# Hybrid pooling/retention layer on eight cores: input tiles moved into the weight queue, and the last tile's work put in another order

## The chip, the cores and the metric

The kernel runs on the 8 cores of one Trainium2 chip. Every core executes the same program on its own data: one prompt of the batch and 16 of the 128 sample rows. There is no exchange between cores. The metric is the device time of the slowest core in microseconds (us); lower is better.

On each core, TensorE (PE) does the matmuls, VectorE (DVE), ScalarE (ACT) and GpSimd (POOL) do the elementwise work, and transfers are issued from two places: from SyncE (SP, "the hardware queue" below) and from POOL ("the software queue" below, which also converts float32 to bfloat16 on the way).

## What is computed

The reference, cut to the prompt part (the sample part is the same layer with one token and a carried state):

```python
hn = rms_norm(h, norm_w)
u, gp, q, k, v, gr = split(hn @ w_in)            # 1024 -> 6 x 1024
# head group A: trailing means over 2/4/8/16 tokens, minus the token, a linear map per group
pool_o = (window_mean(u) - u) @ w_grp * scale
# head group B: retention in chunks of 128, one fixed decay per head
q, k = rotary(q), rotary(k) * HEAD_DIM ** -0.5
scores = (q @ k.T) * dmask
ret_o = scores @ v + q_dec @ S
S = g ** L * S + k_dec.T @ v
ret_y = rms_norm_per_head(ret_o) * ret_norm_w * silu(gr)
h = h + concat([pool_o * silu(gp), ret_y]) @ w_out
y = rms_norm(h, final_norm_w)
```

`w_in` is 1024 x 6144, `w_out` is 2048 x 1024, and a prompt has 2048 tokens after 16 meta tokens.

## The kernel before

A core cuts its 2048 tokens into 16 tiles of 128 (tile 1 to tile 16). Tile 0 is a small one with the 16 meta tokens and the 16 sample rows. `w_in` lies in HBM as 12 blocks of 128 x 4096 float32 and is kept in SBUF as bfloat16; the order in which blocks are loaded is `WORD = (6, 7, 4, 5, 8, 9, 10, 11, 0, 1, 2, 3)`: two blocks each for k, q, v, gr, u and gp. `w_out` is kept as 16 row blocks `wo0` to `wo15`. The first eight come converted through the software queue; the last eight come as float32 through the hardware queue into a float32 buffer and are multiplied by the retention norm weight on DVE (line 537).

For each tile, `stage_A` loads x, normalises it (ACT square at line 581, a power on POOL at line 553, DVE product at line 584) and `turn` transposes it on PE (line 573). `tile_work` then projects k, q, v, gr and u (line 611, 128x512 matmuls, eight for half a projection) and gp (line 626), rotates k and q on DVE (lines 641 to 646), transposes both, forms scores (791), the state update (697), the retention output (806, 808), its norm and gate (ACT 719, DVE 550 and 728, POOL 553), the pooling matmuls (828 to 835), and the mixing matmuls with `wp0` and `wp1` (744). `wp0` and `wp1` are made on DVE (line 517) from `w_pool` and `pool_scale`. `out_proj` (line 758) multiplies by all of `w_out`; then come the residual add (762), the final norm (764, 553, 767) and the store.

The order is not written by hand. `Prog.schedule` plans it: every operation has a priority (lower goes first), a planned duration and the buffers that it opens, and the planner fixes for each engine one list of instructions, which that engine then executes strictly in order, waiting on semaphores. Transfers are planned at a fixed rate for each queue. Buffers come from pools: 33 of bfloat16 (`b2`), 5 of float32 (`b4`: input tiles, residuals, rotary scratch, staged weights), 4 of PSUM, 3 of rotary tables (`cs`). An instruction that needs a buffer still in use waits, and so does all that stands behind it on its engine or queue.

Around the start, the priorities put the first constant piece and all 12 weight blocks on the software queue at once, and the eight `w_out` blocks behind them. x1 goes on the hardware queue at the start; x2, x3 and x4 go there too, each gated on the landing of an early weight block. `pool_scale` and `w_pool` go on the hardware queue after the tenth weight block. At the end, tile 16 is planned like every other tile, with its second half (scores, retention, pooling) 50 behind its projections in priority.

Of the kernel before, what the change touches and what calls it, by code (L numbers as in the profile page):

```python
# [12 lines left out]
NH = 8  # L13
# [36 lines left out]
class Prog:  # L50
# [102 lines left out]
    def schedule(self):  # L153
# [216 lines left out]
LAG = 2  # L370
HPE, KQPE, YPE = 99, range(99), range(99)
# [6 lines left out]
def build_program():  # L378
# [18 lines left out]
    c_bf = din("c_bf", [128, NBF])  # L397
    c_f32 = din("c_f32", [128, NF32])
    c_cs = din("c_cs", [NT + 1, 128, 192])
# [26 lines left out]
    csr = P.sb("csr", [128, 3 * 192], F32)  # L426
# [3 lines left out]
    P.pool("cs", [csr[:, i * 192:(i + 1) * 192] for i in range(3)])  # L430
# [39 lines left out]
    def copy_any(src, src_r, dst, cols, prio, rows=128, bf=False, scol=0, dcol=0, only=None, **kw):  # L470
        def fa(e):
            return e.activation(out=dst.ap[:rows, dcol:dcol + cols], in_=srcap(), func=AF.Copy)  # L472
# [4 lines left out]
        def srcap():  # L477
# [4 lines left out]
                    [(src, src_r)], [dst], prio, **kw)  # L482
# [16 lines left out]
    dma("sw", lambda: cbf.ap[:, 256:NBF], lambda: c_bf[:, 256:NBF], [], [(cbf, "b")], 128 * (NBF - 256) * 4, -771.5, "uniq")  # L499
    CA, CB = (cbf, "a"), (cbf, "b")  # L500
    LASTW = (win, WORD[-1])
    dma("hw", lambda: cs0.ap, lambda: c_cs[0], [], [cs0], 128 * 768, -700, "uniq")
    dma("hw", lambda: cf.ap, lambda: c_f32[:, :], [(win, WORD[0])], [cf], 128 * NF32 * 4, -690, "uniq")
# [4 lines left out]
    def load_wpool():  # L508
        pscale = P.tile("b4", "pscale")
        dma("hw", lambda: pscale.ap, lambda: pool_scale[0:1, :].broadcast_to([128, D]), [(win, WORD[9])], [pscale], 1 << 19, 30)  # L510
        for i in range(2):
            wpf = P.tile("b4", "wpf")
            dma("hw", lambda wpf=wpf: wpf.ap.rearrange("p (g cc d) -> p g cc d", g=2, cc=2),
                lambda i=i: w_pool[2 * i:2 * i + 2].rearrange("g (cc p) d -> p g cc d", p=128), [(win, WORD[9])], [wpf], 1 << 19, 31)
# [681 lines left out]
```

How the kernel before makes its waits and increments, by code:

```python
        def run(e, name):  # L327
            for o in self.order[name]:
                for s, v in waits[o.i]:
                    e.wait_ge(self.sems[s], v)
                o.fn(e).then_inc(self.sems[o.semname], 16 if o.nbytes else 1)
            if name == "sp":
                for k, v in cnt.items():
                    e.wait_ge(self.sems[k], v)
```

## Time and profile before

| | us |
|---|---|
| median of 4 runs (664.06 to 664.47) | 664.23 |
| the profiled execution | 664.06 |
| its span, slowest core | 662.4 |
| spans of the 8 cores | 656.5 to 662.4 |
| PE busy in the span | 578.8 (87%) |
| DVE / ACT / POOL busy | 354.6 / 183.6 / 122.3 |
| chain that ended last: PE / DMA / DVE | 78% / 8% / 8% |

The profiled execution's time is 1.7 us above its span. All times below are us from the start of the span on the slowest core (core 2). PE is the busiest engine by far, but not evenly so: the page's 40 slices of 16.6 us each show where it is not.

### The profile page before, as it was taken

Reading aid. Unit: us, or ns where it says so; the run is one execution under the profiler, and the core shown is the slowest. Engines: PE = TensorE matmul, PEld = TensorE weight load, DVE = VectorE, ACT = ScalarE, POOL = GpSimd, SP = SyncE. Lnnn points to the kernel's source line nnn. Section 1 sums busy time; section 2 is a strip of 40 time slices with the busy share of each in tenths; the row PEclk is TensorE's granted clock in tenths of the full one; section 3 lists DMA queues with packets and bytes.
Section 4 is the critical chain, followed back from the end, with each engine's and each line's share of the span. In section 5 each row is a group of like instructions: output and inputs, shape, how many; then the busy total and the mean of one; then the engine's idle time right before and its main releaser. Section 6 shows DMA issues by size and latency. Waiting matters only on the chain.

```text
span 662.4 us, 12122 instructions; the slowest of 8 cores (656.5 to 662.4 us)
## 1 busy us (share of the span) xinstructions
PE 578.8 (87%) x4834; PEld 337.6 (51%) x4834; DVE 354.6 (54%) x536; ACT 183.6 (28%) x437; POOL 122.3 (18%) x127
## 2 busy tenths in 40 slices
PE   0343799999999999899998999899998999999944
PEld 0121355676545565547473656447473646565631
DVE  2033664436549574855746483836665482838341
ACT  2011112334223231424133333324241432212220
POOL 7010014103013020302131221213030310202000
PEclk9757989999999999899998999899998999999977
DMA  8999998351412220624132232404141331001020
GB/s 160 181 176 199 170 182 172 120 139 65 134 52 88 83 103 1 184 76 180 39 127 103 96 135 69 161 33 159 39 164 67 113 117 38 33 1 64 8 94 32
DMA packets 21750, 68.83 MB, mean 104 GB/s; under 512 B 2479, under 2 KB 6895, under 8 KB 20142
## 3 DMA queue, kind: packets, MB, share of 16 engines
q1 hardware_dynamic: 18238, 52.55, 23.6%
q0 software_dynamic: 3456, 15.50, 14.1%
q8 instruction: 39, 0.64, 0.4%
q14 instruction: 17, 0.14, 0.1%
HBM read 66.05 MB, written 18.41 MB: 128 GB/s over the span
## 4 chain that ended last, share of the span: by engine, by line
PE 78%; DMA 8%; DVE 8%; issue 3%; ACT 1%; POOL 0%; DVEq 0%; POOLq 0%; SPq 0%; ACTq 0%
PE pp L611 37%; PE pp L758 17%; PE pp L626 9%; DMA b<-x 5%; PE pp L573 4%; DMA w_in_bf<-w_in 3%; PE pp L744 2%; PE pp L828 1%; DVE b L728 1%; PE pp L791 1%; DVE pp L644 1%; PE pp L697 1%; DVE b L969 1%; PE pp L856 1%; DVE b L796 1%
## 5 line engine op out<-in xcount | busy, mean ns | idle before, releaser
L611 PE MATMUL pp<-w_in_bf,b 128*128 128x512 bf16 x1280 | 301.8, 390 | 9.2 <-DMA w_in_bf<-w_in 4.5
L611 PEld LDWEIGHTS pp<-w_in_bf,b 128*128 128x128 bf16 x1280 | 123.9, 100 | 156.2 <-issue 27.0
L553 POOL TENSOR_TENSOR small<-small,nh 128x1 f32<-128x1 f32 (+2 forms) x51 | 46.1, 903 | 396.9 <-DVE small L547 300.3
L758 PE MATMUL pp<-b 128*128 128x512 bf16 x512 | 117.1, 389 | 2.0 <-ACT b L472 1.1
L472 ACT ACTIVATE b<-pp 128x1024 bf16<-128x1024 bf16 (+2 forms) x59 | 59.7, 1016 | 125.0 <-PE pp L573 84.8
L758 PEld LDWEIGHTS pp<-b 128*128 128x128 bf16 x512 | 51.1, 100 | 66.0 <-issue 9.2
L573 PE MATMUL pp<-cbf,b 128*128 128x128 bf16 x512 | 40.7, 228 | 46.0 <-DVE b L584 28.6
L626 PEld LDWEIGHTS pp<-b,w_in_bf 128*128 128x128 bf16 x1024 | 58.4, 98 | 3.3
L626 PE MATMUL pp<-b,w_in_bf 128*128 128x128 bf16 x1024 | 60.0, 219 | 0.0
L573 PEld LDWEIGHTS pp<-cbf,b 128*128 128x128 bf16 x512 | 33.3, 102 | 52.3 <-issue 48.7
L762 DVE TENSOR_TENSOR b<-b,pp 128x1024 f32<-128x1024 f32 x16 | 19.5, 1221 | 70.1 <-PE pp L758 70.1
L677 ACT ACTIVATE b<-pp 128x1024 bf16<-128x1024 f32 x32 | 32.7, 1022 | 79.7 <-PE pp L611 40.3
L475 DVE COPY b<-pp 128x1024 bf16<-128x1024 bf16 x33 | 22.7, 687 | 57.9 <-PE pp L573 57.9
L764 ACT ACTIVATE b<-b 128x1024 bf16<-128x1024 f32 x16 | 16.9, 1056 | 131.2 <-DVE b L762 131.2
L705 POOL TENSOR_TENSOR S_f<-S_f,cf 128x1024 f32<-128x1024 f32 x16 | 30.4, 1897 | 102.3 <-DVE S_f L785 76.0
L719 ACT ACTIVATE b<-pp 128x128 bf16<-128x128 f32 x128 | 33.4, 293 | 54.4 <-PE pp L808 54.4
L644 DVE TENSOR_TENSOR pp<-pp,csr 128x1024 f32<-128x1024 f32 (+1 forms) x33 | 39.9, 1212 | 1.9
L646 DVE TENSOR_TENSOR b<-pp,b 128x1024 bf16<-128x1024 f32 x32 | 39.0, 1222 | 2.0
L728 DVE SCALAR_TENSOR_TENSOR b<-pp,small,b 128x128 bf16<-128x128 f32 x128 | 34.4, 342 | 8.1 <-POOL small L553 5.4
L547 DVE TENSOR_SCALAR small<-small 128x1 f32<-128x1 f32 (+1 forms) x35 | 5.2, 148 | 59.8 <-ACT b L581 49.1
L581 ACT ACTIVATE b<-b 128x1024 bf16<-128x1024 f32 (+1 forms) x17 | 17.9, 1053 | 64.8 <-DMA b<-x 64.7
L641 DVE TENSOR_TENSOR b<-pp,csr 128x512 f32<-128x512 f32 (+1 forms) x33 | 22.4, 678 | 16.4 <-PE pp L611 9.7
(93 smaller groups left out, 510.9 us busy)
## 6 DMA issues: line engine op xcount, KB each, us to landing
b<-x SPq DMA_DIRECT2D x32, 512.0 KB, 4.5
w_in_bf<-w_in POOLq DMA_DIRECT2D x12, 1024.0 KB, 46.8
y<-b SPq DMA_DIRECT2D x16, 512.0 KB, 2.8
b<-S_in SPq DMA_DIRECT2D x16, 512.0 KB, 4.4
Ss<-b SPq DMA_DIRECT2D x16, 512.0 KB, 3.2
b<-w_out SPq DMA_DIRECT2D x8, 512.0 KB, 3.7
b<-w_out POOLq DMA_DIRECT2D x8, 256.0 KB, 82.1
csr<-c_cs SPq DMA_DIRECT2D x17, 96.0 KB, 5.4
```

The costliest lines, as they stand in the source:

```text
L472: return e.activation(out=dst.ap[:rows, dcol:dcol + cols], in_=srcap(), func=AF.Copy)
L553: pool(lambda e: e.tensor_tensor(out=rp.ap[:T, 0:n], in0=rs.ap[:T, 0:n], in1=nh.ap[:T, 0:n], op=ALU.pow), [rs, nh], [rp], 0.6 if n == 1 el ...
L573: r = e.transpose(out=pt.ap.bitcast(BF16)[:, h * 128:(h + 1) * 128], in_=src.ap[:, h * 128:(h + 1) * 128], identity=ident)
L611: r = e.matmul(pt.ap[:, nt * 512:(nt + 1) * 512], lhsT=hnT.ap[:, kc * 128:(kc + 1) * 128], rhs=win.ap[:, blk + nt, kc, :], start=(kc == 0) ...
L626: r = e.matmul(pt.ap[:, (4 * nt + fc) * T:(4 * nt + fc + 1) * T], lhsT=win.ap[:, blk + nt, kc, fc * 128:(fc + 1) * 128], rhs=hnT.ap[:, kc ...
L644: dve(lambda e: e.tensor_tensor(out=p4(), in0=p4(), in1=cst.ap[:, 0:64].unsqueeze(1).unsqueeze(1) .broadcast_to([128, n, 2, 64]), op=ALU.m ...
L646: dve(lambda e: e.tensor_tensor(out=out.ap[:, 0:w], in0=pt.ap[:, 0:w], in1=t1.ap[:, 0:w], op=ALU.add), [pt, t1], [out], dve_us(w) + 0.05, ...
L677: act(lambda e: e.activation(out=dst.ap[:, 0:w], in_=pg.ap[:, 0:w], func=AF.Silu), [pg], [dst], act_us(w), prio)
L705: pool(lambda e: e.tensor_tensor(out=S_f.ap.rearrange("p (h d) -> p h d", h=8), in0=S_f.ap.rearrange("p (h d) -> p h d", h=8), in1=gpow.un ...
L719: r = e.activation(out=ry.ap[:, h * 128:(h + 1) * 128], in_=pr.ap[:, h * 128:(h + 1) * 128], func=AF.Square, accum_out=ss.ap[:, h:h + 1])
L728: r = e.scalar_tensor_tensor(out=ry.ap[:, h * 128:(h + 1) * 128], in0=pr.ap[:, h * 128:(h + 1) * 128], scalar=rp.ap[:, h:h + 1], in1=G.ap[ ...
L758: r = e.matmul(po.ap[:, nt * 512:(nt + 1) * 512], lhsT=src.ap[:, (kc % 8) * 128:(kc % 8 + 1) * 128], rhs=wo[kc].ap[:, nt * 512:(nt + 1) * ...
```

## The change

1. The four first input tiles and their rotary tables go through the software queue, in between the weight blocks: x1 before the first block, x2 before the second, x3 before the third, x4 after the fourth. The gates are gone.
2. `pool_scale` and `w_pool` go through the software queue too, behind all weight blocks; the first eight `w_out` blocks stay there, behind those. All of these may be issued from the landing of the sixth block on.
3. The constants `c_bf` arrive as bfloat16 in one piece on the hardware queue, first after x0; the float32 constants and the first table follow there without gates.
4. The rotary table loses its third part (-sin): 128 columns instead of 192, and 5 buffers instead of 3. The first rotary product is now a scalar_tensor_tensor with the scalar -1.
5. The planner's rate for the software queue is 0.34 instead of 0.27 MB/us.
6. Tile 16: its second half gets a priority 60 ahead of its projections instead of 50 behind them, and what follows its retention (u, pooling, gp, mixing, output) is put 60 back. The sample rows' pooling (`small_pool`) goes from priority 80 to 470.
7. `turn`, `norm_gate`, `copy_any` and `out_proj` get parameters (`parts`, `last`) that would split them. No call uses them, so the instructions that they issue are as before.

```diff
-                    rate = 0.27e6 if q == "sw" else 0.2e6
+                    rate = 0.34e6 if q == "sw" else 0.2e6
...
+SWX = (-1, 1, 5, 13)
...
-    csr = P.sb("csr", [128, 3 * 192], F32)
+    csr = P.sb("csr", [128, 5 * 128], F32)
...
-    dma("sw", lambda: cbf.ap[:, 0:256], lambda: c_bf[:, 0:256], [], [(cbf, "a")], 128 * 256 * 4, -990, "uniq")
+    dma("hw", lambda: cbf.ap, lambda: c_bf[:, :], [], [cbf], 128 * NBF * 2, -994.5, "uniq")
+    dma("hw", lambda: cf.ap, lambda: c_f32[:, :], [], [cf], 128 * NF32 * 4, -993, "uniq")
...
+    def sw_prio(k):
+        return k - (900 if k < 12 else 700)
...
-    for k, blk in enumerate(WORD[:4]):
-        load_win(blk, -900 + k)
-    for k, blk in enumerate(WORD[4:]):
-        load_win(blk, -780 + k)
+    for k, blk in enumerate(WORD):
+        load_win(blk, sw_prio(4 * k))
...
-        dma("hw", lambda: pscale.ap, lambda: pool_scale[0:1, :].broadcast_to([128, D]), [(win, WORD[9])], [pscale], 1 << 19, 30)
+        dma("sw", lambda: pscale.ap, lambda: pool_scale[0:1, :].broadcast_to([128, D]), [(win, WORD[5])], [pscale], 1 << 19, sw_prio(50))
...
-            dma("sw", lambda kc=kc: wo[kc].ap, lambda kc=kc: w_out[kc * 128:(kc + 1) * 128, :], [], [wo[kc]], 1 << 19,
-                -770 + kc)
+            dma("sw", lambda kc=kc: wo[kc].ap, lambda kc=kc: w_out[kc * 128:(kc + 1) * 128, :], [(win, WORD[5])], [wo[kc]], 1 << 19,
+                sw_prio(60 + kc))
...
-        gate = [(win, WORD[idx - 2])] if early and idx > 1 else []
-        dma("hw", lambda: xt.ap, lambda: x[(idx - 1) * 128:idx * 128, :], gate, [xt], 1 << 19, prio, after=after)
+        q, px, pc = ("sw", sw_prio(SWX[idx - 1]), sw_prio(SWX[idx - 1] + 0.2)) if idx <= LEAD else ("hw", prio, prio + 0.1)
+        dma(q, lambda: xt.ap, lambda: x[(idx - 1) * 128:idx * 128, :], [], [xt], 1 << 19, px, after=after)
...
-            e.tensor_tensor(out=t4()[:, :, 0, :], in0=p4()[:, :, 1, :], in1=bc(2), op=ALU.mult)
+            e.scalar_tensor_tensor(out=t4()[:, :, 0, :], in0=p4()[:, :, 1, :], scalar=-1.0, in1=bc(1), op0=ALU.mult,
+                                   op1=ALU.mult)
...
+        if c == NT:
+            prio += 60
+            prio1 += 60
         P1_u(c, prio1)
...
-        outs.append((c, tile_work(c, c * 100, c * 100 + 50)))
+        outs.append((c, tile_work(c, c * 100, c * 100 + (50 if c < NT else -60))))
         if c == 1:
-            small_pool(80)
+            small_pool(470)
```

On POOL, at the start of the program, the software queue before. `b` stands for the working buffers, `csr` for the rotary tables, `small` for the norms' statistics:

```order
L454 DMA cbf<-c_bf 128x256
L454 DMA w_in_bf<-w_in 128x4096 x4
L553 TENSOR_TENSOR small<-small,nh 32x1
L454 DMA w_in_bf<-w_in 128x4096 x6
L553 TENSOR_TENSOR small<-small,nh 128x1
L454 DMA w_in_bf<-w_in 128x4096 x2
L454 DMA cbf<-c_bf 128x1040
L454 DMA b<-w_out 128x1024 x5
```

The same place now:

```order
L455 DMA b<-x 128x1024
L455 DMA csr<-c_cs 128x128
L455 DMA w_in_bf<-w_in 128x4096
L455 DMA b<-x 128x1024
L455 DMA csr<-c_cs 128x128
L455 DMA w_in_bf<-w_in 128x4096
L455 DMA b<-x 128x1024
L455 DMA csr<-c_cs 128x128
L455 DMA w_in_bf<-w_in 128x4096
L557 TENSOR_TENSOR small<-small,nh 32x1
L557 TENSOR_TENSOR small<-small,nh 128x1
L455 DMA w_in_bf<-w_in 128x4096
```

The first three input tiles and their tables now stand ahead of the first three blocks; behind the fourth block come x4, its table, the other eight blocks, `pool_scale`, `w_pool` twice, and `w_out` eight times.

On PE, the stretch in which the gp projections of tiles 0, 1 and 2 stand (they use the last two weight blocks; `smp` is tile 0's input). Before:

```order
L626 MATMUL pp<-smp,w_in_bf 128x32 x32
L626 MATMUL pp<-b,w_in_bf 128x128 x64
L626 MATMUL pp<-smp,w_in_bf 128x32 x32
L626 MATMUL pp<-b,w_in_bf 128x128 x32
L828 MATMUL pp<-cbf,b 128x128
```

The same stretch now, up to the first mixing matmuls (L755, on `wp0` and `wp1`):

```order
L632 MATMUL pp<-smp,w_in_bf 128x32 x32
L632 MATMUL pp<-b,w_in_bf 128x128 x64
L580 MATMUL pp<-cbf,b 128x128 x8
L632 MATMUL pp<-smp,w_in_bf 128x32 x32
L632 MATMUL pp<-b,w_in_bf 128x128 x64
L821 MATMUL pp<-b 128x128 x8
L755 MATMUL pp<-b 128x128 x16
```

Before this stretch stand, in the changed kernel, the k, q, v, gr and u projections of tiles 1 and 2 and the k and q of tile 3; v of tile 3, which stood ahead of it before, now stands behind it, with gr, u and gp of tile 3 and all of tile 4 as before. From tile 5's gp to tile 16's q the PE list is the same in both kernels.

On PE, near the end, after the retention output of tile 15. Before:

```order
L611 MATMUL pp<-w_in_bf,b 128x512 x48
L573 MATMUL pp<-cbf,b 128x128 x8
L611 MATMUL pp<-w_in_bf,b 128x512 x8
L758 MATMUL pp<-b 128x512 x32
L611 MATMUL pp<-w_in_bf,b 128x512 x8
L626 MATMUL pp<-b,w_in_bf 128x128 x64
L697 MATMUL pp<-b 128x128 x8
L573 MATMUL pp<-cbf,b 128x128 x16
```

The same place now (L772 is the output projection, of tile 15 here):

```order
L617 MATMUL pp<-w_in_bf,b 128x512 x16
L580 MATMUL pp<-cbf,b 128x128 x8
L617 MATMUL pp<-w_in_bf,b 128x512 x24
L580 MATMUL pp<-cbf,b 128x128 x8
L617 MATMUL pp<-w_in_bf,b 128x512 x8
L580 MATMUL pp<-cbf,b 128x128 x8
L704 MATMUL pp<-b 128x128 x8
L772 MATMUL pp<-b 128x512 x16
L821 MATMUL pp<-b 128x128 x8
L772 MATMUL pp<-b 128x512 x16
```

The transposes of k and q, the state update and the scores of tile 16 now stand among its projections and tile 15's output projection. Behind this come tile 16's retention output, its u projection, half of gp, the pooling, the other half of gp, the transpose of the gated retention output, the mixing and the last output projection.

## Rows read from the trace of the kernel before

**Rows 1.** The page: PE's busy tenths in 40 slices of the span.
```profile
PE   0343799999999999899998999899998999999944
```
**Rows 2.** Busy time by stretch: us, then busy us of each engine, clock, DMA, GB/s.
```profile
core 2: us, PE busy (x) PEld busy (x) DVE busy (x) ACT busy (x) POOL busy (x), PEclk, DMA share, GB/s
23.00:40.00 17.00, 2.38 (x8) 0.64 (x7) 0.89 (x2) 1.15 (x2) 1.40 (x3) 0.53 1.02 186
66.00:92.00 26.00, 21.52 (x128) 8.87 (x126) 15.61 (x20) 3.47 (x5) 0.55 (x1) 0.82 1.01 171
92.00:178.20 86.20, 84.03 (x905) 55.24 (x906) 44.87 (x67) 26.37 (x70) 18.22 (x13) 1.00 0.53 134
199.00:624.00 425.00, 411.84 (x3428) 241.88 (x3426) 259.82 (x400) 130.20 (x316) 84.22 (x76) 0.98 0.25 88
629.00:643.00 14.00, 5.41 (x82) 4.58 (x79) 7.29 (x14) 4.79 (x19) 1.65 (x1) 0.84 0.33 114
643.00:653.00 10.00, 9.83 (x32) 3.61 (x32) 0.07 (x1) 0.00 (x0) 0.00 (x0) 0.72 0.01 2
```
**Rows 3.** Timeline, PE, ACT and POOL at the start: start, length, instruction [idle before <-releaser].
```profile
12.28 1.12 POOL L454 DMA_DIRECT2D w_in_bf<-w_in  x2
...
17.08 3.57 PE L611 MATMUL pp<-w_in_bf,b 128*128 128x512 bf16 x8 [2.22 <-DMA w_in_bf<-w_in]
...
37.05 1.06 ACT L581 ACTIVATE b<-b 128x1024 bf16<-128x1024 f32 x1 [25.71 <-DMA b<-x]
...
58.51 1.06 ACT L581 ACTIVATE b<-b 128x1024 bf16<-128x1024 f32 x1 [15.68 <-DMA b<-x]
```
**Rows 4.** Issues one by one: transfer, queue, KB, us from issue to landing.
```profile
w_in_bf<-w_in POOLq DMA_DIRECT2D x1, 1024.0 KB, 78.7
...
b<-x SPq DMA_DIRECT2D x1, 512.0 KB, 19.6
...
b<-x SPq DMA_DIRECT2D x1, 512.0 KB, 35.2
...
b<-w_pool SPq DMA_DIRECT2D x1, 512.0 KB, 21.1
...
finw_b<-finw SPq DMA_DIRECT2D x1, 512.0 KB, 21.6
...
b<-w_out SPq DMA_DIRECT2D x1, 512.0 KB, 3.7
```
**Rows 5.** The chain that ended last, from 136 us to the first output projections.
```profile
136.09 0.89 PE pp L744 x16
...
149.98 0.89 PE pp L573 x16
...
156.95 6.91 PE pp L611 x32
...
174.66 3.57 PE pp L626 x64
178.23 20.80 PE pp L758 x96
```
**Rows 6.** The same chain, from tile 15's retention output to the end.
```profile
603.82 10.36 PE pp L611 x48
...
634.31 2.19 ACT b L719 x16
636.91 1.66 POOL small L553
638.66 2.17 DVE b L728 x8
...
642.93 9.91 PE pp L758 x32
652.93 1.23 DVE b L762
```
**Rows 7.** Groups of DVE by form: count, busy us, mean ns, idle before.
```profile
L641 DVE TENSOR_TENSOR b<-pp,csr 128x512 f32<-128x512 f32 x32 | 21.9, 686 | 13.3 <-PE pp L611 9.7 <-DMA csr<-c_cs 3.5
L969 DVE SCALAR_TENSOR_TENSOR b<-b,pp 128x512 f32<-128x512 f32 x32 | 20.4, 679 | 0.2
```

More of the change, by code:

```diff
@@ L429, in build_program @@
     P.pool("b4", [b4[:, i * D:(i + 1) * D] for i in range(NB4)])
-    P.pool("cs", [csr[:, i * 192:(i + 1) * 192] for i in range(3)])
+    P.pool("cs", [csr[:, i * 128:(i + 1) * 128] for i in range(5)])
     P.pool("ps", [t[:] for t in pp])
@@ L568, in turn, with tr @@
         pt = P.tile("ps", "tr")
-        def tr(e):
-            r = None
-            for h in range(8):
-                r = e.transpose(out=pt.ap.bitcast(BF16)[:, h * 128:(h + 1) * 128],
-                                in_=src.ap[:, h * 128:(h + 1) * 128], identity=ident)
-            return r
-        pe(tr, [src, CA], [pt], mm_us(8, 128), prio)
-        copy_any(pt, None, dst, D, prio, bf=True)
+        n = 8 // parts
+        for k in range(parts):
+            key = k if parts > 1 else None
+            def tr(e, k=k):
+                r = None
+                for h in range(k * n, (k + 1) * n):
+                    r = e.transpose(out=pt.ap.bitcast(BF16)[:, k * 1024 + (h - k * n) * 128:
+                                                            k * 1024 + (h - k * n + 1) * 128],
+                                    in_=src.ap[:, h * 128:(h + 1) * 128], identity=ident)
+                return r
+            pe(tr, [(src, key), CA], [(pt, key)], mm_us(n, 128), prio + 0.1 * k)
+            copy_any(pt, key, (dst, key), n * 128, prio + 0.1 * k, bf=True, scol=k * 1024, dcol=k * n * 128)
     def normed(T, xt, hn, prio):
@@ L749, in mix, with out_proj, mm @@
             [pm, sg], [yp], dve_us(8 * T) + 0.06, prio)
-    def out_proj(yp, yr, xr, prio, store):
+    def out_proj(yp, yr, xr, prio, store, last=False):
         po = P.tile("ps", "out")
-        for nt in range(2):
-            def mm(e, nt=nt):
+        groups = [(nt, 0, 16) for nt in range(2)]
+        if last:
+            groups = [(0, 0, 8), (1, 0, 8), (0, 8, 16), (1, 8, 16)]
+        for n, (nt, k0, k1) in enumerate(groups):
+            def mm(e, nt=nt, k0=k0, k1=k1):
                 r = None
-                for kc in range(16):
+                for kc in range(k0, k1):
                     src = yp if kc < 8 else yr
@@ L769, in out_proj @@
-        return dma("hw", lambda: store, lambda: xr.ap, [xr], [], 1 << 19, prio)
+            pe(mm, ([yp] if k0 == 0 else []) + ([yr] if k1 == 16 else []) + wo, [(po, nt)], mm_us(k1 - k0, 512), prio + 0.01 * n)
+        parts = 2 if last else 1
+        w = D // parts
+        sc = [col(1) for _ in range(parts)]
+        for k in range(parts):
+            key = k if last else None
+            cs = slice(k * w, (k + 1) * w)
+            dve(lambda e, cs=cs: e.tensor_tensor(out=xr.ap[:, cs], in0=xr.ap[:, cs], in1=po.ap[:, cs], op=ALU.add),
+                [(xr, key), (po, key)], [(xr, key)], dve_us(w) + 0.06, prio)
+            act(lambda e, cs=cs, k=k: e.activation(out=yp.ap[:, cs], in_=xr.ap[:, cs], func=AF.Square,
+                                                   accum_out=sc[k].ap[:, 0:1]), [(xr, key)], [sc[k], (yp, key)], w / 1024 + 0.25, prio)
@@ new lines, in out_proj @@
+        if last:
+            dve(lambda e: e.tensor_tensor(out=sc[0].ap[:, 0:1], in0=sc[0].ap[:, 0:1], in1=sc[1].ap[:, 0:1], op=ALU.add),
+                sc, [sc[0]], 0.1, prio)
+        rp = rstd(128, 1, sc[0], None, prio, inv_n=1.0 / D)
+        r = None
+        for k in range(parts):
+            key = k if last else None
+            cs = slice(k * w, (k + 1) * w)
+            dve(lambda e, cs=cs: e.scalar_tensor_tensor(out=xr.ap[:, cs], in0=xr.ap[:, cs], scalar=rp.ap[:, 0:1],
+                                                        in1=finw_b.ap[:, cs], op0=ALU.mult, op1=ALU.mult),
+                [(xr, key), rp, finw_b], [(xr, key)], dve_us(w) + 0.1, prio)
+            r = dma("hw", lambda cs=cs: store[:, cs], lambda cs=cs: xr.ap[:, cs], [(xr, key)], [], (1 << 19) // parts, prio,
+                    "uniq" if last else None)
@@ L771, in tile_work @@
+        return r
     def tile_work(c, prio1, prio):
@@ L1146, in _constants @@
             b[32 * j + 16 + s, C_SEL + s] = 1.0
-    c["c_bf"] = b
+    c["c_bf"] = b.astype(mybir.dt.np(BF16))
     return c
```

75 lines of the change are left out of this document (34 added, 41 removed).

## The prediction, made before the changed kernel ran

> **What bounds the kernel now.** I read the page's slices first, then busy time by stretch, then the chain that ended last, and only then single issues. PE is busy to nine tenths or more from the seventh slice to the third from the end; what it loses lies in the first five or six slices and in the last two [rows 1]. The stretches say how much. From 199 to 624 us PE is busy 411.8 of 425 us at a granted clock of 0.98 [rows 2]: there is little to win there. From 23 to 40 us it works 2.4 of 17 us while the DMA engines are full (share 1.02). From 66 to 92 us it works 21.5 of 26 us, at a granted clock of 0.82. From 629 to 643 us it works 5.4 of 14 us, and the last output projection behind that runs at 0.72 [rows 2].
>
> In the start two things arrive late. The first weight block ends PE's first wait at 17.1 us. After that ACT waits 25.7 us for x2, until 37.0, and again 15.7 us for x3, until 58.5 [rows 3]. These tiles are issued on the hardware queue while the software queue is full of weights, and take 19.6 and 35.2 us to land; a `w_out` block of the same 512 KB, issued later, takes 3.7 [rows 4]. So weight blocks lie in SBUF without an x to multiply them. The last weight block is the second of the pair issued from 12.28 to 13.40 us, so it is issued at about 12.8, and it lands 78.7 us later, at 91.5 [rows 3, 4]. By then PE is far behind: the chain shows the first mixing matmuls only at 136.1 us and the first output projection at 178.2 us, with 84.0 of 86.2 us busy in between at full clock [rows 2, 5].
>
> At the end the chain leaves PE: tile 16's retention output goes through ACT (2.19), POOL (1.66) and DVE (2.17) before the last output projection can start, and nothing else is left for PE to do. That projection takes 9.91 us where the three at 178.2 take 20.80, or 6.93 each [rows 5, 6].
>
> **Start, weights and x.** Nothing is removed from what must land: the same 12 blocks and four x tiles, now in one line, each x just ahead of the block that it is needed for. From the first block (17.1 us) to the last (91.5), 11 blocks of 1.05 MB and three x tiles of 0.52 MB landed, 13.1 MB in 74.4 us. With both queues at work the rows have 186 GB/s, with the software queue almost alone 171 [rows 2]. One line of 13.1 MB at 171 is 76.6 us. Ahead of the first block stand as before x0, the norm weight and x1, and now the whole of `c_bf` in bfloat16, 332 KB in place of 64: 1.5 us at 171 to 186. So the last block lands between 91.5 us (no change) and 17.1 + 1.5 + 76.6 = 95.2; I take 93.5. What is moved past on POOL: the powers for x2, x3 and x4 stand behind 6, 12 and 12 blocks' issues, which are 0.56 us each (1.12 for two, rows 3), and while POOL waits for them the queue holds 15 us or more of weights.
>
> Will PE keep up with the weights? Its list up to the last two blocks holds k, q, v, gr and u of two tiles (10 pairs of 3.46 us, from 6.91 for 32 matmuls), k and q of tile 3 (6.9), half of two gp (3.6) [rows 5], and about 15 us of transposes, retention and small passes, counted in the list at the same matmul rate: 60 us, for the 76 from 17.5 to 93.5. Each block now meets 3.5 to 5 us of work in its 6 to 7 us. I take it that PE ends each block's work before the next lands, and that the last block ends the wait.
>
> **Start, what is left after the last weight.** From the first mixing matmuls to the first output projection the old list took 178.2 - 136.1 = 42.1 us [rows 5]. The new list has, from the last block on, this work and besides it: the second halves of three gp (4.4 us), tile 2's scores and retention output (1.35), v of tile 3 (3.46), and tile 4's state update, two transposes and pooling (2.0; a transpose pair is 0.89, rows 5), less the sample rows' mixing (0.4). That is 52.9 us.
>
> A new wait stands in it. `w_pool` now comes behind the last weight: 1.57 MB with `pool_scale`, 8.4 to 9.2 us at 186 to 171 GB/s, and with the final norm weight and a first staged `w_out` block beside it on the hardware queue 2.6 MB, 14 to 15 us. DVE's product adds some 1.5 us (1.2, twice the 512-column form of rows 7, and its start). PE has 4.9 us of work (the gp halves and the scores), then it stands at the mixing matmuls, and with it everything behind; on DVE the score mask of tile 2 stands behind the product. So PE waits 5 to 12 us; the row of `w_pool` before, 21.1 us with others beside it [rows 4], gives 17.7 as an upper end. I take 7, nearer to the bare transfer, because this queue now has `w_pool` first. Right behind stand DVE's products for `wo8` and `wo9`, whose loads share the engines with eight other `w_out` blocks: 0 to 5 us more, I take 2. So 9 us of waiting, 5 to 20.
>
> First output projection: 93.5 + 52.9 + 9 = 155.4 us. The old one stood at 178.2, with 1.6 us of this work still to do. The start gives 178.2 + 1.6 - 155.4 = **24.4 us**; by the bounds 30 down to 12. The later `w_out` blocks are tied to float32 buffers that tile 4's rotary frees, as before, so they move along with PE.
>
> **The middle.** From tile 5 on the lists are the same. The product with -1 changes 33 instructions from a tensor_tensor of 686 ns to a scalar_tensor_tensor; the nearest row of that shape has 679 ns [rows 7]. DVE is off the path: nothing. The smaller tables save a third of small transfers that nobody waits for late: nothing.
>
> **The end.** The work is the same, in another order: tile 16's scores and transposes go in among its projections (10.36 us) and tile 15's output projection, and u, gp and pooling fill the time in which ACT, POOL and DVE take 2.19 + 1.66 + 2.17 us [rows 6] for the gate. PE idles 14.0 - 5.4 = 8.6 us today, and loses 9.9 - 6.9 = 3.0 us to the clock: at most 11.6 us. Behind the retention output PE has u (3.46), gp (3.57) and pooling (0.6), 7.6 us, to cover 6.0 us and three hand-overs. What stays is the mixing product on DVE (1.2 us and its start) ahead of the last projection, 1.5 us. So **10 us**; 6 if the short wait costs the clock again. The residual, the norm and the store from 652.9 on stay as they are.
>
> **Sum.** 664.06 (the profiled execution, 0.17 below the median) - 24.4 - 10 = 629.7 us.
>
> **What speaks against it.** The hardware queue takes 19.6 and 35.2 us for an x under the weights [rows 4]. The Trainium skill (DMA: Bandwidth & Descriptors, "Issuing engine by pattern") gives simple loads to the Sync engine, as the generally faster way; by that rule this change goes the wrong way, and x would be no earlier. The rows say otherwise as long as weights fill the other queue.
>
> PE worked at a granted clock of 0.53 in the stretch from 23 to 40 us, after waits for x and weights, 0.82 from 66 to 92, and 1.00 once it no longer waited [rows 2]. The Trainium skill (TensorE: Matmul & The Clock Gate, "HAM oscillation — how this bites in real kernels") describes a kernel that waited on DMA ahead of every weight slice and ran each slice at the low one of the two levels. By that rule the clock rival below would hold; the stretch from 66 to 92 us speaks half for it.
>
> **Rivals.**
> *Late small weights.* The wait for `w_pool` and the staged `w_out` blocks costs 20 to 30 us instead of 9: 641 to 651 us. For it: 21.1 and 21.6 us for such transfers in company [rows 4], and in-order lists that put DVE's `wo8` and `wo9` products ahead of tile 3's v. Against: half of that company is now behind them in the same line. 0.17.
> *Slow clock, slower in the end.* Each block's work is short and followed by a wait, so PE stays at 1.2 GHz until the last weight. The 60 us of work become 120 from 17.5 us on, PE reaches the last block's work at 137 instead of 93.5, and the time is 629.7 + 43.5 = 673 us. It turns into a loss where the mean granted clock in that stretch falls below 60 / (76 + 34.4) = 0.54. For it the 0.53 of 23 to 40 us; against it the 0.82 that 21.5 of 26 us busy gave, and that work stretched by a lower clock closes its own gaps. 0.04.
> *x no earlier.* The tiles take as long in the software queue as they did beside it; only the end gains: 654 us. For it only that no x went this way before; against it that blocks there land every 6 to 7 us in the order of issue. 0.04.
>
> **Numbers.** My forecast, 620 to 641 us, has 0.71; the three rivals 0.17, 0.04 and 0.04; 0.04 is for a better start still. By the bounds the forecast reaches from 664.1 - 30.4 - 11.6 = 622 to 664.1 - 11.5 - 6 = 647. The range 620 to 647 holds the forecast and somewhat over half of the first rival. About 0.2% is what a measurement of this kernel can tell from no change; faster by more 0.94, within it 0.01, slower by more 0.05.
>
> **What would show it.** PE should run with gaps under 6 us from 23 us on, ACT's waits for x should be over by 50 us, and the last weight should still land at 91 to 96 us. A wait of 5 to 12 us should stand ahead of the first mixing matmuls near 100 us, released by DVE, and the first output projection should start at 150 to 160 us. The last output projection should start 8 us or less after the PE work ahead of it and take 7 us. The prediction is wrong if the last weight lands after 100 us, if the granted clock up to 90 us is below 0.6, or if PE stands for 20 us or more between 95 and 155 us.

## The result, and the profile after

The changed kernel takes **629.46 us** (median of 8 runs, 628.71 to 632.11) against 664.26 (13 runs beside it): ratio 0.948, 95% interval 0.947 to 0.950. The prediction was 629.7 us, with a range of 620 to 647, which holds it. Now and then an execution runs slow (one of the 13 of before, 737.32 us, and two of the five of the run with later `w_out` below, 663.97 and 708.59, there with the cores of one die at a lower granted clock), and all ratios leave such executions out. The profiled execution took 630.42 us with a span of 628.9 on core 6; all rows of after are of that core, the slowest of the eight (619.0 to 628.9).

PE's busy tenths in 40 slices of 15.7 us, to hold against [rows 1]:

```profile
PE   0789998599999999899998999799998998999994
```

The second to the fifth slice, 3, 4, 3 and 7 before, now read 7, 8, 9 and 9. One dip is left, the 5 in the eighth slice (110 to 126 us), and the weak end is one slice long instead of two. By stretch, in the columns of [rows 2]:

```profile
core 6: us, PE busy (x) PEld busy (x) DVE busy (x) ACT busy (x) POOL busy (x), PEclk, DMA share, GB/s
23.00:40.00 17.00, 13.65 (x63) 5.91 (x62) 9.15 (x11) 2.17 (x3) 2.00 (x4) 0.80 1.00 192
66.00:92.00 26.00, 24.47 (x225) 14.64 (x227) 9.04 (x15) 7.72 (x23) 7.62 (x6) 0.95 1.01 172
93.50:158.70 65.20, 55.90 (x608) 39.58 (x611) 35.26 (x50) 16.47 (x45) 9.86 (x8) 0.97 0.66 161
176.00:601.00 425.00, 407.71 (x3400) 242.13 (x3440) 259.51 (x399) 134.13 (x322) 81.91 (x76) 0.99 0.26 90
596.00:613.50 17.50, 15.74 (x169) 10.94 (x169) 7.96 (x16) 7.29 (x22) 2.17 (x2) 1.00 0.31 96
613.50:620.50 7.00, 6.85 (x31) 2.93 (x30) 0.00 (x0) 0.00 (x0) 0.00 (x0) 1.00 0.00 1
```

From 23 to 40 us PE works 13.65 us instead of 2.38, and the last output projection runs at full clock in 6.85 us instead of 9.91 [rows 6]. The reason for the first stands in ACT's waits for x (timeline of ACT; in brackets the idle time before and what ended it), where [rows 3] had 25.71 and 15.68 us:

```profile
9.59 1.06 ACT L589 ACTIVATE b<-b 128x1024 bf16<-128x1024 f32 x1 [3.73 <-DMA b<-x]
19.12 1.06 ACT L589 ACTIVATE b<-b 128x1024 bf16<-128x1024 f32 x1 [5.73 <-DMA b<-x]
27.52 1.06 ACT L589 ACTIVATE b<-b 128x1024 bf16<-128x1024 f32 x1 [7.25 <-DMA b<-x]
42.14 1.06 ACT L589 ACTIVATE b<-b 128x1024 bf16<-128x1024 f32 x1 [0.97 <-DMA b<-x]
```

Each row starts some 0.1 us after a tile's landing: x1 to x4 land at 9.5, 19.0, 27.4 and 42.1 us, where they landed at 10.1, 37.0, 58.4 and 66.1. The last weight block is issued at 23.84 and takes 69.61 us, so it lands at 93.45. Behind it PE still waits, in these places (timeline of PE; the first row is the gp projection just ahead of the last block's first matmuls, the second row is these, and neither has a wait ahead of it):

```profile
89.27 5.36 PE L632 MATMUL pp<-b,w_in_bf 128*128 128x128 bf16 x64
...
94.92 0.95 PE L632 MATMUL pp<-smp,w_in_bf 128*128 128x32 bf16 x32
...
101.57 1.05 PE L755 MATMUL pp<-b 128*128 128x128 bf16 x16 [1.68 <-DVE b L521]
...
115.45 0.61 PE L580 MATMUL pp<-cbf,b 128*128 128x128 bf16 x8 [3.49 <-DVE b L739]
...
122.63 5.36 PE L632 MATMUL pp<-b,w_in_bf 128*128 128x128 bf16 x64 [3.12 <-DVE b L666]
...
159.09 21.72 PE L772 MATMUL pp<-b 128*128 128x512 bf16 x94 [0.69 <-DVE b L479]
```

L521 is the `w_pool` product. Lines 739 and 666 are DVE work that stood behind the products of the staged `w_out` blocks (L541); DVE's waits from 90 to 160 us (us in total, times, longest) show that:

```profile
DVE b L541 <- DMA b<-w_out: 12.8, 3, 6.4
...
DVE b L521 <- DMA b<-w_pool: 3.0, 2, 1.5
```

The last row of PE above is the first output projection (a few records of it are missing, so it began near 158.7). At the end, the gate of tile 16 on POOL and DVE (1.64 and 2.16 us) now runs under PE's u, gp and pooling; only the mixing product is waited for:

```profile
607.21 2.16 DVE L739 SCALAR_TENSOR_TENSOR b<-pp,small,b 128x128 bf16<-128x128 f32 x8 [0.88 <-POOL small L557]
...
613.55 6.85 PE L772 MATMUL pp<-b 128*128 128x512 bf16 x31 [1.76 <-DVE b L759]
620.51 1.22 DVE L782 TENSOR_TENSOR b<-b,pp 128x1024 f32<-128x1024 f32 x1 [7.32 <-PE pp L772]
```

### The profile page after: what moved, and what is told of

It is laid out like the page before. It is cut to its first block, busy times and chain, and to the rows that moved or that the text cites. A ratio compares the mean times of both kernels' runs of the same rounds, so it can differ in the third digit from the quotient of the medians.

```text
span 628.9 us, 12074 instructions; the slowest of 8 cores (619.0 to 628.9 us)
## 1 busy us (share of the span) xinstructions
PE 567.3 (90%) x4776; PEld 337.0 (54%) x4834; DVE 354.2 (56%) x534; ACT 184.8 (29%) x439; POOL 128.7 (20%) x136
## 4 chain that ended last, share of the span: by engine, by line
PE 73%; DVE 7%; another core or an unknown queue 7%; DMA 6%; issue 3%; ACT 1%; SPq 0%; POOL 0%; DVEq 0%; POOLq 0%; ACTq 0%
PE pp L617 36%; PE pp L772 18%; PE pp L632 8%; PE pp L580 4%; DMA b<-x 2%; DMA b<-w_out 2%; DMA pbs<-b 2%; PE pp L755 2%; PE pp L821 1%; DVE b L1002 1%; DVE b L739 1%; PE pp L861 1%; DVE b L479 1%; DVE b L759 1%
## 5 line engine op out<-in xcount | busy, mean ns | idle before, releaser
L617 PE MATMUL pp<-w_in_bf,b 128*128 128x512 bf16 x1235 | 290.4, 387 | 12.9 <-DMA w_in_bf<-w_in 3.5
L772 PE MATMUL pp<-b 128*128 128x512 bf16 x499 | 113.6, 383 | 4.3 <-DVE b L759 1.8
L772 PEld LDWEIGHTS pp<-b 128*128 128x128 bf16 x512 | 50.3, 99 | 64.3 <-issue 6.8
L632 PE MATMUL pp<-b,w_in_bf 128*128 128x128 bf16 x1024 | 63.2, 225 | 3.1 <-DVE b L666 3.1
L632 PEld LDWEIGHTS pp<-b,w_in_bf 128*128 128x128 bf16 x1024 | 61.6, 101 | 6.7 <-issue 3.6
L782 DVE TENSOR_TENSOR b<-b,pp 128x1024 f32<-128x1024 f32 x16 | 19.5, 1221 | 63.0 <-PE pp L772 63.0
L580 PE MATMUL pp<-cbf,b 128*128 128x128 bf16 x512 | 38.8, 221 | 14.2 <-DVE rT L1023 5.2
L580 PEld LDWEIGHTS pp<-cbf,b 128*128 128x128 bf16 x512 | 31.7, 99 | 21.4 <-issue 17.4
L647 DVE SCALAR_TENSOR_TENSOR b<-pp,csr 128x512 f32<-128x512 f32 (+1 forms) x33 | 22.4, 678 | 14.6 <-PE pp L617 14.4
L826 DVE TENSOR_TENSOR b<-pp,cbf 128x1024 bf16<-128x1024 f32 x16 | 19.6, 1222 | 19.4 <-PE pp L821 19.4
L730 ACT ACTIVATION_READ_ACCUMULATOR b<-pp 128x1 f32 x128 | 28.6, 223 | 0.0
```

Source lines behind the costliest of these rows:

```text
L580: r = e.transpose(out=pt.ap.bitcast(BF16)[:, k * 1024 + (h - k * n) * 128: k * 1024 + (h - k * n + 1) * 128], in_=src.ap[:, h * 128:(h + 1 ...
L617: r = e.matmul(pt.ap[:, nt * 512:(nt + 1) * 512], lhsT=hnT.ap[:, kc * 128:(kc + 1) * 128], rhs=win.ap[:, blk + nt, kc, :], start=(kc == 0) ...
L632: r = e.matmul(pt.ap[:, (4 * nt + fc) * T:(4 * nt + fc + 1) * T], lhsT=win.ap[:, blk + nt, kc, fc * 128:(fc + 1) * 128], rhs=hnT.ap[:, kc ...
L730: r = e.activation(out=ry.ap[:, h * 128:(h + 1) * 128], in_=pr.ap[:, h * 128:(h + 1) * 128], func=AF.Square, accum_out=ss.ap[:, h - h0:h - ...
L772: r = e.matmul(po.ap[:, nt * 512:(nt + 1) * 512], lhsT=src.ap[:, (kc % 8) * 128:(kc % 8 + 1) * 128], rhs=wo[kc].ap[:, nt * 512:(nt + 1) * ...
```

## The experiments

The theory after the result: the start gains because x no longer waits on the hardware queue, the end because tile 16's gate is covered. The rival for the start: it is not x but the constants, or `w_pool`, or merely which queue x uses. In edits of the planned lists below, `take` removes the transfers of the named tiles from an engine's list and `put` inserts them at a position (`sp` is the hardware queue, `pool` the software queue); everything else keeps its place.

**The two halves apart.** The kernel before with tile 16's priorities alone:

```diff
+        if c == NT:
+            prio += 60
+            prio1 += 60
...
-        outs.append((c, tile_work(c, c * 100, c * 100 + 50)))
+        outs.append((c, tile_work(c, c * 100, c * 100 + (50 if c < NT else -60))))
```

> The kernel before with the change to tile 16's priorities alone (its start, constants and transfers are as before). Theory: the two halves of the change add up, and the end is worth what the two traces show between tile 15's retention output and the end of the last output projection, 49.0 against 38.2 us, so 10.8 us, and 1 us behind it: 652 to 654 us. Rival: the end only gains because the start is early (PE, DMA or buffers in another state): 660 us or more.

Measured 653.51 us (653.12 to 654.06), ratio 0.985 (0.983 to 0.986): 10.4 us. And the kernel after with these lines taken back:

> The changed kernel with tile 16's priorities as in the kernel before. Theory: only the end's 11 to 12 us are lost: 640 to 642 us, with the first output projection again near 159 us. Rival: the halves overlap, and more than 3 us either way are missing from the sum.

Measured 638.35 us (635.98 to 641.28), ratio 0.962 (0.959 to 0.965): 25.6 us, a little better than expected. The two sum to 36.0 where both together gave 34.8: they add up within the spread.

**x back on the hardware queue, in after's lists.** First with x2 to x4 behind the landing of an early block, as before; then with all four free from the start:

```diff
     P.schedule()
+    for i in (4, 3, 2, 1):
+        got = take("pool", ("x%d" % i, "cs%d" % i))
+        put("sp", 5, got)
+        for o in got:
+            if o.bufs[0].name[0] == "x" and i > 1:
+                o.deps[wld[i - 2].i] = "raw"
```

> The changed kernel with the same instruction lists on PE, DVE, ACT and POOL, but x1 to x4 and their tables issued on the hardware queue, x2 to x4 each after the landing of the first, second and third weight block, as before. Theory (late x tiles are what the old start lost): x3 and x4 land at 55 to 68 us, PE stands for them, the later waits for staged w_out blocks shrink in return, and the first output projection comes 7 to 17 us later: 637 to 647 us. Rival (the new order of the lists, the constants or the pool weights' place give the gain): within 2 us of the changed kernel, 628 to 632 us.

Measured 638.41 us (637.92 to 638.78), ratio 0.961 (0.960 to 0.963): 9 us of the gain lost. The time lies in the theory's range and excludes the rival, but the way there was another: x3 and x4 landed at 33.5 and 35.0 us, not at 55 to 68. What came late was x1, at 29.4 us behind constants and a table, so PE's first matmul stood at 32.43 us instead of 12.55. On POOL the power for x1 stands ahead of the fourth weight block; it waited as well, the software queue was empty from 27.6 to 32.5 us, and in that gap the other x tiles landed quickly.

```diff
     P.schedule()
+    for i in (4, 3, 2, 1):
+        put("sp", 5 if i > 1 else 2, take("pool", ("x%d" % i, "cs%d" % i)))
```

> The changed kernel with the same lists, but x1 to x4 and their tables issued on the hardware queue at the start, without any gate. Theory (it counts when an x lands, not which queue brings it): four x land by about 35 us beside the first two weight blocks, the last weight still lands near 93.5 us, and the time is 628 to 633 us. Rival (the hardware queue itself is slow beside the weights, 19.6 to 36 us for an x as in the kernel before, one behind the other): x4 lands after 60 us and the time is 636 us or more.

Measured 653.61 us (651.62 to 655.92), ratio 0.985 (0.982 to 0.987): the theory missed by 20 us, and the time lies on the rival's side. PE waits for the norm weight until 30 us and then for x2 (timeline of PE of this run):

```profile
54.18 1.01 PE L580 MATMUL pp<-cbf,b 128*128 128x128 bf16 x8 [17.05 <-DVE b L592]
```

The landings show why. Between the landings of the first blocks, at 14.8, 21.7, 28.6, 35.5, 42.8 and 50.3 us, the hardware queue landed exactly one transfer each: x1 (15.0), a 64 KB table (21.9), the norm weight (28.8), 18 KB of constants (35.7), a table (43.0), x2 (50.5). The small transfers took as long as the large ones. The packets of the two queues say what a turn is (the view of the queues of this run, from 22 to 28.8 us: packets, MB, share):

```profile
q0 software_dynamic: 143, 1.04, 82.5%
q1 hardware_dynamic: 142, 0.46, 20.7%
```

In the next turn, from 28.8 to 35.7 us, with the 18 KB of constants:

```profile
q0 software_dynamic: 145, 1.06, 93.8%
q1 hardware_dynamic: 144, 0.02, 3.2%
```

One packet of the hardware queue goes for one of the software queue, whether the 144 packets carry 0.46 or 0.02 MB. The kernel before already did so (30 to 43 us):

```profile
q0 software_dynamic: 280, 2.03, 90.1%
q1 hardware_dynamic: 279, 0.42, 11.0%
```

So there x2 was late because tables and constants, 128 rows each, stood ahead of it and took a weight block's time apiece.

**The test of that.** The run before, with the small transfers (and the tables of x1 to x4) on the software queue; with them gone, the norm weight stands third on the hardware queue and x1 to x4 right behind it:

```diff
     P.schedule()
+    small_hw = [o for o in od["sp"] if o.nbytes in (128 * NF32 * 4, 1 << 16) and o.prio in (-993, -992)]
+    od["sp"] = [o for o in od["sp"] if o not in small_hw]
+    xs = take("pool", ("x1", "x2", "x3", "x4"))
+    put("pool", 0, small_hw)
+    put("sp", 3, xs)
```

> The kernel after with x1 to x4 on the hardware queue, ungated and right behind x0, c_bf and the norm weight; all small transfers that stood ahead of them there (float32 constants, tables 0 to 4) go into the software queue between the weight blocks. It is the run with free x tiles (653.6 us) with only the small transfers changed over. Theory A (while the software queue holds weight blocks, the hardware queue lands one transfer for each block, whatever its size, so small transfers ahead of x cost as much as large ones): x1 lands at 15 to 22 us, x2 to x4 each one block (7 us) later, about 22 to 43 us in all, and the time is 628 to 636 us, close to after. Theory B (large transfers on the hardware queue are starved beside the software queue by their bytes): x2 to x4 land at 40 us or later, and the time is 645 us or above.

Measured 631.18 us (628.93 to 632.62), ratio 0.951 (0.948 to 0.953). x1 to x4 landed at 11.4, 18.7, 25.8 and 32.2 us. The time and x2 to x4 are as theory A had them; x1 came earlier than its 15 to 22 us. So 22 us lie between this run and the one before, from what stands ahead of x on the same queue (small transfers out of the way, norm weight ahead of x1). The next run asks whether the turn is a transfer or a row:

```diff
+    for n, o in zip((1, 2, 3, 4), xs):
...
+        o.fn = lambda e, n=n, xb=xb: e.dma_start(out=xb.ap[0:64], in_=x[(n - 1) * 128:(n - 1) * 128 + 64, :])
+        o2.fn = lambda e, n=n, xb=xb: e.dma_start(out=xb.ap[64:128], in_=x[(n - 1) * 128 + 64:n * 128, :])
```

> The run with x first on the hardware queue (631.2 us; x2, x3, x4 landed at 18.7, 25.8 and 32.2 us, one for each weight block), with each of x1 to x4 cut into two transfers of 64 rows; rows, bytes and order are the same. It asks what a turn beside the software queue is counted in. Theory A (in transfers): a half lands for each block, so x2 is whole at about 25 us, x3 at 39, x4 at 52, PE stands without x3 while weights are there, and the time is 638 to 652 us. Theory B (in rows, 128 for 128): two halves land for each block, x2 to x4 at 18 to 34 us as before, and the time is 629 to 634 us.

Measured 632.44 us (629.63 to 633.96), ratio 0.952 (0.950 to 0.955). The tiles were whole at 13.2, 19.6, 28.0 and 35.4 us, x4 a little behind theory B's 34, far from theory A's 39 and 52 for x3 and x4: rows, theory B. From 19 to 31 us the queues again moved the same number of packets:

```profile
q0 software_dynamic: 247, 1.67, 82.4%
q1 hardware_dynamic: 246, 0.80, 20.3%
```

**x alone.** The kernel before, with x1 to x4, the tables of x1 and x2 and POOL's power for x1 moved into or within the software queue's list and nothing else:

```diff
     P.schedule()
+    for i in (3, 2, 1):
+        got = take("sp", ("x%d" % i,) + (("cs%d" % i,) if i < 3 else ()))
...
+        put("pool", od["pool"].index(wld[i - 1]), got)
...
+    put("pool", k, r1 + x4)
```

> The kernel before, its planned lists kept, with one thing moved: x1, x2, x3 go into the software queue ahead of the first, second and third weight block (with the tables of x1 and x2), x4 after the fourth. Constants, small tables, w_pool, w_out, the PE order and tile 16 stay as before. Theory (what held the start was the landing of x2 to x4 at 37, 58 and 66 us, because each waited its turn behind small transfers of the hardware queue): x2 to x4 land at about 19 to 43 us, the first output projection starts 15 to 24 us earlier than before's 178.2, and the time is 641 to 650 us. Rival (the gain of the start needs the constants, the table order and w_pool in the software queue too): x1 is early, but its rotation waits for the first constants and tables, which still land at 43 us or later on the hardware queue; the time stays at 656 or above.

Measured 651.23 us (650.00 to 651.96), ratio 0.981 (0.980 to 0.983). Theory and rival both missed, by 1.2 and 4.8 us, and the time lies in between: x landed as in after (10.7, 19.5, 28.7, 42.4 us), but the first output projection moved only to 168.4 us, and the gain is 12 of the start's 25.6 us. Of what is still missing, the trace shows `w_pool` on the hardware queue, which landed at 104.3 and 112.4 us; PE waited 5.6 and 4.4 us for DVE in the stretch in which DVE waited for it (waits of DVE, 5 to 180 us):

```profile
DVE b L517 <- DMA b<-w_pool: 19.7, 2, 13.9
```

**w_pool alone.** After, with `pool_scale` and `w_pool` on the hardware queue:

```diff
     P.schedule()
+    got = take("pool", ("pscale", "wpf"))
+    for o in got:
+        o.deps[wld[9].i] = "raw"
+    put("sp", fin[0], got)
```

> The kernel after with pool_scale and w_pool (each w_pool transfer is 512 rows of 1 KB) moved from the software to the hardware queue, behind the tenth weight block as in the kernel before; all else stays. Theory A (turns counted in transfers): pool_scale lands with the eleventh block at 87 us, w_pool with the twelfth and with the first w_out block, 93 to 97 us, and the time is 627 to 631 us. Theory B (turns counted in rows, so that a w_pool transfer takes four turns, as the 9.0 and 8.2 us between landings in the run with x alone in the software queue suggest): w_pool lands at about 100 and 110 us, PE waits some 8 us more ahead of the mixing, and the time is 635 to 642 us, in the direction of the prediction's rival of late small weights.

Measured 638.04 us (637.39 to 638.31), ratio 0.961 (0.960 to 0.963): theory B. `w_pool` landed at 101.9 and 110.0 us, each in the turns of four 128-row transfers, and PE stood for it (timeline of PE):

```profile
111.60 1.87 PE L755 MATMUL pp<-b 128*128 128x128 bf16 x16 [12.98 <-DVE b L521]
```

The packets of the two queues in this run, from 94 to 110 us:

```profile
q0 software_dynamic: 1065, 1.91, 69.7%
q1 hardware_dynamic: 1073, 1.45, 32.9%
```

So `w_pool` and `pool_scale` in the software queue are worth 8.6 us of the change. With the 12 us of x alone that leaves, if they add up, some 5 of the start's 25.6 us, which I did not test one by one, for the constants, the table order and the planner's new lists.

**The constants' form.** The kernel before with the new rotary product and the smaller tables:

```diff
-    csr = P.sb("csr", [128, 3 * 192], F32)
+    csr = P.sb("csr", [128, 3 * 128], F32)
...
-            e.tensor_tensor(out=t4()[:, :, 0, :], in0=p4()[:, :, 1, :], in1=bc(2), op=ALU.mult)
+            e.scalar_tensor_tensor(out=t4()[:, :, 0, :], in0=p4()[:, :, 1, :], scalar=-1.0, in1=bc(1), op0=ALU.mult, op1=ALU.mult)
```

> The kernel before with the new rotary product alone: scalar_tensor_tensor with -1 and tables of 128 columns instead of 192; every engine's list is the same. Theory (DVE is off the path, and the smaller tables arrive no sooner because a transfer takes its turn whatever its size): within 0.2% of before, 662.0 to 665.6 us. Rival (a third fewer table bytes on the hardware queue let x2 to x4 land earlier): 1 us or more below before.

Measured 663.41 us beside 664.13, ratio 0.9992 (0.9980 to 1.0005): no change.

**The waits that are left.** After, with `wo0` to `wo7` issued behind the first pooling transfers; then also with the staged `w_out` loads first on the hardware queue:

```diff
     P.schedule()
+    got = take("pool", tuple("wo%d" % i for i in range(8)))
+    k = [j for j, o in enumerate(od["pool"]) if o.bufs and o.bufs[0].name.startswith("spb")][-1]
+    put("pool", k + 2, got)
```

> The kernel after with the eight w_out transfers of the software queue issued later (behind the pooling powers of the first tiles on POOL), so that they no longer run beside the staged w_out loads of the hardware queue. Theory (the 12.8 us that DVE waited for staged w_out, and through it PE in its waits of 3.49 and 3.12 us, came from sharing with the software queue): the staged loads land in 3 to 6 us instead of 13 to 15, the two PE waits shrink, and the time is 623 to 627 us. Rival (PE has other late inputs behind these, or the later wo0 to wo7 become late themselves): within 1.5 us of after's 629.5, or above.

Measured 624.77 us (three runs, 624.63 to 624.84), ratio 0.942 (0.940 to 0.944), 4.7 us better than after. The theory held in the time and in the waits; the staged loads came sooner, but the first four took 7 to 10 us and not 3 to 6. The waits of PE from 90 to 160 us are gone but for two hand-overs, and DVE's for staged `w_out` fell from 12.8 to 2.7 us:

```profile
PE pp L772 <- DVE b L479: 0.7, 1, 0.7
PE pp L580 <- ACT b L476: 0.4, 1, 0.4
...
DVE b L541 <- DMA b<-w_out: 2.7, 3, 2.0
```

The gp projection that took 5.36 us at 122.6 us in after has no wait ahead of it here, and takes 3.74 (timeline of PE):

```profile
114.99 3.74 PE L632 MATMUL pp<-b,w_in_bf 128*128 128x128 bf16 x64
```

```diff
+    put("sp", w[-1] + 1, fin)
+    put("sp", w[4] + 1, xr)
+    put("sp", w[0] + 1, uf[:2])
```

> As the run with later w_out transfers, and on the hardware queue the staged w_out loads are also issued ahead of the final norm weight, the sample rows' pooled history and the first two residual tiles. Theory: the staged loads land first of all, DVE's waits for them are gone, and the time is 621 to 626 us, up to 2 us below the run that only has the software transfers later. Rival (what was put behind becomes late: the residual tiles stand ahead of the first two output tiles): no better than that run, or above 629.5.

Measured 624.04 us (621.17 to 629.38), ratio 0.942 (0.936 to 0.948): not to be told from the run before it. The run with later `w_out` beats the changed kernel clearly; for this one, with its wide spread, the two intervals just touch (0.948 and 0.947).

**All together.** The last run combines these, with the first weight block ahead of everything on the software queue:

```diff
+    put("pool", 1, cs1 + small_hw[::-1])
+    put("sp", 3, xs)
```

> The kernel after with what the runs taught put together: the first weight block is the first transfer of the software queue, x1 to x4 are on the hardware queue right behind x0, c_bf and the norm weight (one lands for each 128 rows of the software queue), all small transfers stand between the weight blocks on the software queue, and w_out is ordered as in the run with the staged loads first (624.0 us). Theory: the first block lands at about 15 us instead of 17.6, the staged w_out loads are in time, the last weight still lands at 92 to 94 us because the sum of bytes is the same, so the time is 621 to 625 us, no more than 3 us below the run with the staged loads first. Rival (weights land earlier all the way, and the start moves with them): 618 to 621 us.

Measured 626.64 us (625.40 to 629.02), ratio 0.945 (0.943 to 0.947): a miss. The first block landed at 14.6 us, but the norm weight, third on the hardware queue, now shared its turn with that block's rows and landed at 14.8 us, x1 at 19.0; in the run with the small transfers first they landed at 8.4 and 11.4. PE had nothing to do before 22 us (timeline of PE):

```profile
22.03 0.37 PE L904 MATMUL pp<-cbf,b 32*128 32x32 bf16 x8 [22.03 <-DVE b L592]
...
25.79 3.57 PE L617 MATMUL pp<-w_in_bf,b 128*128 128x512 bf16 x8 [1.05 <-DVE b L479]
```

My reading: where small transfers go first on the software queue, their rows pass in little time and the hardware queue's turns with them; beside the weights' 16 KB rows each turn is long. This run changes several things at once and has no twin that changes one, so the reading is argued from the landings, not shown by itself. The landings of the runs side by side (us, issue plus time to landing):

| kernel | x1 | x2 | x3 | x4 | last weight | time |
|---|---|---|---|---|---|---|
| before | 10.1 | 37.0 | 58.4 | 66.1 | 91.6 | 664.26 |
| after | 9.5 | 19.0 | 27.4 | 42.1 | 93.5 | 629.46 |
| x gated, hardware queue | 29.4 | 32.1 | 33.5 | 35.0 | 95.1 | 638.41 |
| x free, behind small transfers | 15.0 | 50.5 | 51.8 | 53.2 | 95.9 | 653.61 |
| x free, small transfers moved | 11.4 | 18.7 | 25.8 | 32.2 | 92.8 | 631.18 |
| the same in halves | 13.2 | 19.6 | 28.0 | 35.4 | 91.9 | 632.44 |
| x alone moved | 10.7 | 19.5 | 28.7 | 42.4 | 96.5 | 651.23 |
| all together | 19.0 | 26.9 | 34.3 | 41.5 | 91.8 | 626.64 |

## Why the prediction was right

**The last weight** was put at 93.5 us and landed at 93.45.

**PE keeps pace** nearly held: the last block's first matmuls began at 94.9, 1.5 us late, and that was the clock: the gp projection ahead of them took 5.36 us, with the granted clock at 0.74 from 88.4 to 95 us, where the run with later `w_out` has 3.73. The slow-clock rival fell: from 17 to 92 us PE was busy 66.3 of 75 us at a granted clock of 0.94. That oscillation, which the Trainium skill (TensorE: Matmul & The Clock Gate, "HAM oscillation — how this bites in real kernels") describes for work cut up by DMA waits, did not come here; 0.80 from 23 to 40 us, where 0.5 would be the lower level (1.2 GHz) throughout, is the most that is seen of it.

**Left after the last weight** were predicted 52.9 us of work and 9 us of waiting. From 93.5 to 158.7 us PE was busy 55.9 of 65.2 and idle 9.3. The 3.0 us too much are the 1.5 us of late work and, once more, matmuls at the lower clock: the gp projection at 122.6 us took 5.36 us (granted clock 0.79 from 122 to 130) where the run with later `w_out` has 3.74. It stood behind a wait and the one at 89.3 did not, so a wait alone does not explain either. So the first output projection stood at 158.7 instead of 155.4, and the start gave 178.2 + 1.6 - 158.7 = 21.1 us in the profiled execution, for 24.4 predicted; the run of the start alone gave 25.6 in the medians. Core 6, the slowest, is the latest of the eight here: the others have their first matmul of this projection on record at 152.9 to 156.6 us, and by the medians of the eight cores (176.7 before, 154.6 after) the start gave 22.1 + 1.6 = 23.7 us.

**The waiting was right in sum by luck, and wrong in its parts**: this is the step that failed. `w_pool` was put at 7 us (5 to 12) and cost 1.7; `wo8` and `wo9` were put at 2 us (0 to 5) and cost 6.6 (3.49 + 3.12). The working let the queues share by bytes. `w_pool` had hardly anything to share with: it and `pool_scale` landed 6.6 us after the last weight, for 8.4 to 9.2 in the working without company, because the hardware queue's transfers, issued from 93.5 us on, moved next to nothing at first (packets of the two queues from 94.64 to 100 us):

```profile
q0 software_dynamic: 360, 0.91, 87.2%
q1 hardware_dynamic: 69, 0.28, 16.9%
```

So the mixing matmuls stood at 101.6 us, 3.8 sooner than put (93.5 + 4.9 + 7 = 105.4), and PE was ready for them 1.5 us later than put; that makes 1.7 of the 7. A staged `w_out` block, on the other hand, had three or four transfers ahead of it in its own queue, each with its turns beside `wo0` to `wo7`, and the first four took 13 to 15 us (from 100 to 125.5 us):

```profile
q0 software_dynamic: 1167, 2.08, 55.3%
q1 hardware_dynamic: 1082, 3.76, 47.4%
```

The run with later `w_out` transfers shows this side, the run with `w_pool` on the hardware queue the other: there it took the turns of 512 rows for each transfer, while in the software queue the 360 packets above are far fewer than the 1024 rows of its two. The rival of late small weights points at that run: 13.0 us of waiting in one place and 638.04 us, short of the rival's 20 to 30 and 641 to 651. The change avoids this by its own second part.

**Nothing in the middle** held: tile by tile the lists took 423.5 us from the first output projection to tile 15's retention output, with 1.6 us less work in them, against 425.6; the run of the rotary product showed no change. That nobody waits for the tables was too much said, as [rows 7] have DVE waiting 3.5 us for one; by that run, smaller tables do not help.

**The end** was put at 10 us. From tile 15's retention output to the end of the last projection it took 49.0 us before and 38.2 after: 10.8, with a wait of 1.76 us for 1.5 predicted, 6.85 us of matmuls for 6.9, and 10.4 us in the medians by itself.

**The sum** came within 0.3 us of the median, which is luck too: in the profiled executions the start gave 3.3 us less than put, the end 0.8, the middle 0.5 and what follows the last projection 1.2 more, and the execution profiled lies 1.0 above its median.

**x no earlier** fell, but the rule set against the change, the Trainium skill's preference for the Sync engine in simple loads (DMA: Bandwidth & Descriptors, "Issuing engine by pattern"), did not fall with it: x on the hardware queue gave 631.18 us when no small transfer stood ahead of it, and 653.61 when some did. What counts in these runs is the line ahead, not the queue. My reading of [rows 4], that x is slow beside the weights, took the queue for the cause.

Later `w_out` transfers moved the first output projection by 9.3 us (159.1 to 149.8) but the last one only by 6.0 (613.55 to 607.54). The clock accounts for the difference: between the two projections the granted clock stood at 0.5, the lower level, for 12.4 us in after's trace and for 19.0 us in that run's, and 6.6 us more at half speed are 3.3 us of work by my estimate. Why it fell more often there is open; over the eight cores of either execution this time varies from 3.4 to 20.5 us.

## What to carry to other kernels

Beside a full queue, price a transfer of the other queue by the packets it moves (here about one for each row) and by those ahead of it, not by its bytes: put what PE needs next ahead of every small table, or let the small ones ride in the full queue. Compare the packet counts of the two queues in a stretch before deciding that a queue is slow. When the last tile's tail runs through other engines, keep some of PE's own work to put beneath it.

## What the runs showed of the hardware

While both queues were filled, the hardware queue's packets went one for one with those of the software queue: 142 to 143, 144 to 145, 279 to 280 and 246 to 247 beside weights, 1073 to 1065 beside `w_out`, with 0.02 to 1.45 MB in them. A 128-row transfer is about 144 of these packets, so in the run with x free the 512 KB of the norm weight took 6.9 us (21.9 to 28.8) and the 18 KB of constants behind them 6.9 as well (28.8 to 35.7). The counts part where a queue runs out or has only begun: 426 to 100 from 43.0 to 50.3 us of that run, when the last of the blocks issued so far ran out, and 69 to 360 in after from 94.64 to 100 (above). They are not exact in every stretch: from 97 to 110 us of after they are 448 to 600. Once the software queue was empty, from 50.3 us, the next four transfers behind x2 landed within 2.8 us. The Trainium skill (DMA: Bandwidth & Descriptors, "Queues, rings and completion order") says that each DMA engine goes round robin between its queues packet by packet; the equal counts agree.
